# Half as many places for projection slices in the RWKV chunk chain and in the attention core

## What is computed

```python
x = half_swiglu(x, ffn1...)
h = rmsnorm(x, mix_norm)
proj = h @ w_in                    # attention q/k/v of 3 groups | RWKV r,k,v,lora | 2 gates
# attention: 3 dilated groups, 8 heads of 64, QK-norm, ALiBi, softmax, combined by log-sum-exp
# RWKV-7: a scan over time with a 64x64 state per head
#   S = S * w - sk (kk a)^T + v k^T ;  o = S r
x = x + (sigmoid(gA) * (o_attn @ w_branch_attn) + sigmoid(gR) * (o_rwkv @ w_branch_rwkv)) @ w_out
x = half_swiglu(x, ffn2...)
```

## Time and profile before

| | us |
|---|---|
| median of 3 runs | 1797.46 |
| lowest and highest | 1797.06, 1799.55 |
| the profiled execution: device time | 1800.92 |
| its span, first to last instruction | 1799.1 |
| PE busy in it | 1752.8 (97%) |
| PEld busy (weight loads) | 1671.7 (93%) |
| DVE, ACT, POOL busy | 682.3, 631.4, 684.3 |
| mean granted TensorE clock | 0.989 |

### The profile page before, as it was taken

One profiled execution on the slowest core, in us unless ns is written; L12 is line 12 of the kernel. 1 busy time (PEld: TensorE's weight loads), 2 busy tenths in 40 slices (PEclk: granted clock), 3 DMA queues, 4 the chain that ended last, 5 costly groups with the idle time before them and its releaser, 6 DMA issues.

```text
span 1799.1 us, 41814 instructions
## 1 busy us (share of the span) xinstructions
PE 1752.8 (97%) x17024; PEld 1671.7 (93%) x17024; DVE 682.3 (38%) x1113; ACT 631.4 (35%) x825; POOL 684.3 (38%) x816
## 2 busy tenths in 40 slices
PE   6999999999899999999999999999999999999999
PEld 5999999999799999998788989898899999999999
DVE  5222012223764545453573443527444222012210
ACT  5222122233533333332253434435234443144421
POOL 3555445544422222220132323224255555445543
PEclk9999999999899999998899999999999999999999
DMA  4343333332442334231054454546443344333343
GB/s 168 117 128 125 109 114 117 128 129 79 174 146 98 101 108 150 82 113 54 31 216 168 178 180 166 180 142 237 154 158 125 121 124 130 107 123 117 128 134 123
DMA packets 53113, 237.51 MB, mean 132 GB/s; under 512 B 7040, under 2 KB 7680, under 8 KB 51584
## 3 DMA queue, kind: packets, MB, share of 16 engines
q1 hardware_dynamic: 45120, 219.40, 35.8%
q10 hardware_dynamic: 7872, 16.37, 2.5%
HBM read 217.98 MB, written 71.76 MB: 161 GB/s over the span
## 4 chain that ended last, share of the span: by engine, by line
PE 60%; issue 21%; POOL 14%; DVE 2%; ACT 2%; DVEq 0%; POOLq 0%; ACTq 0%
PE ps L355 43%; POOL w_lo L342 14%; PE ps L819 3%; PE ps L1757 1%; PE ps L1934 1%; PE ps L1802 1%; ACT w_hi L335 1%; PE ps L1872 1%; PE ps L1858 1%; PE ps L1842 1%; PE ps L1878 0%; PE ps L965 0%; PE ps L939 0%; PE ps L935 0%; ACT qkv L1545 0%
## 5 line engine op out<-in xcount | busy, mean ns | idle before, releaser
L342 POOL TENSOR_TENSOR w_lo<-w_raw,w_hi 128x256 fp32r<-128x256 f32 (+1 forms) x808 | 678.6, 872 | 1098.8 <-ACT w_hi L335 1098.8
L355 PE MATMUL ps<-h_hi,w_hi 128*128 128x288 f32 x2432 | 546.7, 307 | 22.4 <-POOL w_lo L342 17.8
L355 PE MATMUL ps<-h_lo,w_hi 128*128 128x288 f32 x2432 | 522.6, 297 | 0.0
L355 PE MATMUL ps<-h_hi,w_lo 128*128 128x288 f32 x2432 | 522.5, 297 | 0.0
L355 PEld LDWEIGHTS ps<-h_hi,w_hi 128*128 128x128 f32 x2432 | 393.5, 190 | 45.1 <-issue 25.5
L335 ACT ACTIVATE w_hi<-w_raw 128x1024 fp32r<-128x1024 f32 (+1 forms) x204 | 226.6, 1111 | 586.6 <-PE ps L355 575.8
L355 PEld LDWEIGHTS ps<-h_lo,w_hi 128*128 128x128 f32 x2432 | 394.2, 190 | 0.0
L355 PEld LDWEIGHTS ps<-h_hi,w_lo 128*128 128x128 f32 x2432 | 393.6, 190 | 0.0
L355 PE MATMUL ps<-g_lo,w_hi 128*128 128x288 f32 x704 | 151.2, 296 | 0.0
L355 PE MATMUL ps<-g_hi,w_hi 128*128 128x288 f32 x704 | 151.0, 296 | 0.0
L355 PE MATMUL ps<-g_hi,w_lo 128*128 128x288 f32 x704 | 151.0, 296 | 0.0
(11 more groups left out here) (368 smaller groups left out, 1915.4 us busy)
## 6 DMA issues: line engine op xcount, KB each, us to landing
w_raw<-in_w SPq DMA_DIRECT2D x172, 512.0 KB, 3.3
w_raw<-in_w SPq DMA_DIRECT2D x32, 704.0 KB, 4.1
kv<-in_kc SPq DMA_DIRECT2D x32, 576.0 KB, 6.1
kv<-in_vc SPq DMA_DIRECT2D x32, 576.0 KB, 7.0
cache_out<-in_cache SPq DMA_DIRECT2D x28, 576.0 KB
gates<-gate_out ACTq DMA_DIRECT2D x16, 288.0 KB, 2.6
cache_out<-in_cache SPq DMA_DIRECT2D x8, 480.0 KB
kvT<-qkv ACTq DMA_DIRECT2D x4, 864.0 KB, 4.4
```

Source lines behind the costliest of these rows:

```text
L342: last = nc.gpsimd.tensor_tensor(w_lo[par_][:, c], w_raw[par_][:, c], w_hi[par_][:, c].bitcast(F32), ALU.subtract)
L355: last = nc.tensor.matmul(ps[:, b + c, 0:HC], w[par_][:, wk], a[:, k, c * HC:(c + 1) * HC], start=(first and k == 0), stop=(end and k == n ...
```

## The change

Two tables change. In the chunk chain the eight places of one slice become four places of two: before step 1 and after steps 2, 4 and 6; after steps 1, 3, 5 and 7 nothing is issued. In the attention core, for pairs 0 to 2, slots 0, 2, 4 and 6 get all eight slices of an ahead unit in place of six, and slots 1, 3, 5 and 7 none in place of two. Slots 8 and 9, the whole of pair 3 and every other place stay. No instruction is added or taken away; the order on TensorE alone changes.

```diff
 AHEAD = 5
-SLOTS = ((6, 2, 6, 2, 6, 2, 6, 2, 3, 5),) * 3 + ((4, 4, 4, 4, 4, 4, 4, 4, 0, 0),)
+SLOTS = ((8, 0, 8, 0, 8, 0, 8, 0, 3, 5),) * 3 + ((4, 4, 4, 4, 4, 4, 4, 4, 0, 0),)
 NORMS = (0, 3, 5, 4, 6, 7)
 
 FILL = {"norm": (1, 4, 4, 4), "tokens": (2, 3, 5, 2), "bonus": 1, "products": 2, "level": (5, 3, 3, 3, 3), "mv": 4, "xk": 3,
-        "chunk": (1, 1, 1, 1, 1, 1, 1, 1), "tail": (3, 2)}
+        "chunk": (2, 0, 2, 0, 2, 0, 2, 0), "tail": (3, 2)}
```

## The result

| | median us | lowest, highest | runs |
|---|---|---|---|
| kernel before | 1800.3 | 1794.64, 1806.13 | 20 |
| changed kernel | 1805.01 | 1800.75, 1812.63 | 20 |

The ratio is 1.0026, with a 95% interval of 1.0015 to 1.0037: 2.7 to 6.7 us slower, 4.7 between the medians. The forecast difference of +3.7 us (1.0021) lies inside that interval, but the forecast time, 1801.2 us in a range up to 1804.3, misses the measured 1805.01. The two halves of that sentence are what the rest is about.

The account below looks back on a forecast made before the run. TensorE's own stream was taken to bound the kernel. Three tiles gave -0.2 us and three pairs +3.9, together +3.7 on the median 1797.46: 1801.2 us, range 1797.4 to 1804.3.

Parts of the forecast that it names:

- slot 1: Attention core, mix(0) directly after scores(2): no wait, 0.7 us to spare before scores(3); +0.02 us a pair.
- slot 3: Attention core, mix(2) waits 0.53 us for ScalarE's copy for head 0; with 0.02 for slices, +0.55 us a pair.
- slot 5: Attention core: two consecutive waits on ScalarE's copies, first 0.5 us, second adding 0.4; +0.93 us a pair with slices.
- slot 7: Attention core: the halves, lines 1940 and 1934, touch without slices between; -0.19 us a pair, 0 if the join costs more.
- chunk chain, a tile: Tiles 0 to 2: four appended slices +3.20, removed ones -1.58, -0.63, -1.07; sum -0.08 us, bounds -0.2 and +0.2.
- the join after step 7: Chunk chain, two blocks of the same 64x64 shape meet: 1.08 us for 36 matmuls (1.01 to 1.30), so -1.07.
- Step 6: Chunk chain: after step 5 without its slice, 0.81 us to the next step; a 0.16 wait for VectorE surfaces.
- the case's own bounds: Forecast case, waits show as priced: 1799.3 to 1803 us, chance 0.64, half slower and half same.
- Absorbed: Rival: waits coincide with existing ones, ScalarE answers sooner, or first loads precede the wait's end; 1798.9 us, chance 0.13.
- Faster by saved switches: Rival: each of the vanished runs in chunk chains and core saves idle time at tile-shape changes; 1793.2 us, chance 0.06.
- A further wait: Rival: a wait at slot 1 or for a unit's split weights, 1.2 us a pair or less; 1802 to 1804.5, chance 0.07.
- The clock at slot 7: Rival: clock falls in 5.7 us of lines 1934 and 1940 without a slice; 1803 to 1806 us, chance 0.10.

Follow-up runs that it names:

- e5: Kernel before with only slots 2 and 3 changed to eight slices and none: pairs 53.38, 53.32, 53.36 us, +0.61.
- e6: Kernel before with only slots 4 and 5 changed to eight slices and none: pairs 53.70, 53.72, 53.68 us, +0.96.
- e7: Kernel before with only slots 6 and 7 changed to eight slices and none: pairs 52.54, 52.48, 52.52 us, -0.23.
- e2: Kernel before with only the chunk chain's new places: tiles 19.71 us, median 1798.55, ratio 0.9987 [0.9972, 1.0002].
- e9: Kernel before with slots 4 and 5 at eight and none, ScalarE's copy of ahead unit 2 moved up: pairs 53.08, 52.98, 53.05 us, +0.30.
- e10: Kernel before with slots 2 and 3 at eight and none, ScalarE's copy of turn(2) done twice: pairs 55.56, 55.56, 55.48 us.
- e3: Changed kernel again, on the same chip as its two parts, against the kernel before: median of 10 runs 1803.94 us, ratio 1.0022 [1.0008, 1.0036].

## Why the prediction was right and wrong

**The direction and the size of the difference: right.** Forecast +3.7, measured 4.7 [2.7, 6.7], and +3.7 by the distances: 3 x (54.11 - 52.74) - 3 x 0.15.

**The terms of the sum.**

| | forecast | shown | by |
|---|---|---|---|
| slot 1, a pair | +0.02 | +0.03 | the rest of the whole |
| slot 3 | +0.55 | +0.61 | e5 |
| slot 5 | +0.93 | +0.96 | e6 |
| slot 7 | -0.19 | -0.23 | e7 |
| chunk chain, a tile | -0.08 | -0.15 | changed kernel, e2 |

In slot 3 the latency after the copy was 0.11 and not the 0.06 that a VectorE instruction showed. In the chunk chain the join after step 7 took 1.02 in place of 1.08, and an appended slice 0.79 in place of 0.80. Step 6 took 0.84 after step 5 (567.22 to 568.06), not 0.81, since the step that starts behind slices begins 0.02 slower. Both waits of slot 5 were found where they were put, one behind the other, and e9 took the second away alone. The second was priced a little low: it idled 0.67, of which 0.16 had stood there before, so 0.5 was new and not 0.4. In the prediction the case's own bounds are also added up a little too wide: three tiles of -0.2 to +0.2 and three pairs of 0.9 to 1.6 give 1799.6 to 1802.9, not 1799.3 to 1803.

**The time itself: wrong.** The step that failed is the one that put the difference "on the median: 1797.46 + 3.7 = 1801.2". I read a median of three runs, within 2.5 us of each other, as the kernel's level. Twenty runs gave 1800.3 and a range of 11.5, so the level was 2.8 too low, and 1800.3 + 3.7 would have been 1804.0, inside the range. The warning was on the page: the profiled execution was 3.5 above that median. I noted it and dropped it. The bounds of the forecast's case then were made from the terms of the change alone, with nothing for the level they stood on. A part of the miss is bad luck: of all sets of three that can be drawn from those twenty runs, 6% have a median 2.8 or more off 1800.3. But the runs shown gave no reason to trust the level to a microsecond.

**The rivals.** Absorbed: no, each of twelve pairs is longer. Faster by saved switches: only slot 7 and the end of the chunk chain save one, as those rows said. A further wait: none at slot 1, and none for split weights at slot 2. The clock at slot 7: it didn't fall, in the changed kernel or in e7. But the clock was a rival at the wrong place. In the seven profiles with slot 7 empty it never fell along line 1934; where it fell in a pair, in e10, a wait of 1.2 us had gone before, which is not shown to be the cause. In none of the twelve pairs of the changed kernel did it do so, with waits of 0.58 and of 0.49 and 0.67.

**The rule beside the row.** That a wait holds the load too was right: at 568.06 and at 983.54 the loads idle for VectorE and ScalarE. The pull-ahead of weight loads that the Trainium skill tells of (TensorE: Matmul & The Clock Gate, "Architectural detail") was not seen to pass a wait here.

**Open.** The medians differ by 1.0 more than the distances, and that is within the interval; in the second comparison (e3) they differ by 3.7, as the distances do. No profile showed anything in the changed places that would explain more. The changed kernel's seven slowest timed runs (1808.48 to 1812.63) lie above every run of the kernel before beside them (up to 1806.13), and none of them has a profile. Their mean granted clock over the whole span is on record, 0.988 to 0.990, against 0.989 to 0.992 in the seven fastest (1800.75 to 1802.5). So they stood longer at the lower clock. By the two means, 0.9887 and 0.9909, that is an estimated 4 us of the 9 between the groups. Where in the span it was, and whether the new waits had a part in it, is neither shown nor excluded.

## What to carry to other kernels

Where filling stands between a producer and the block that waits for its result, it is a cover with a size: measure when the result is ready after the block that starts it, and leave at least that much filling there. In this kernel the joins at the other places cost nothing that shows, and where one spared a change of tile shape it gave back 0.2 to 0.3 us. Look for waits that queue on the engine that answers: a copy behind two others can cost more than the one being waited for. Before a forecast is made in absolute time, ask how far whole executions differ, and where the level of the shown runs stands beside the profiled one; for changes of a few us, compare distances between the same instructions rather than spans.

## What the runs showed of the hardware

In one execution the granted clock fell to 0.51 (1.2 GHz) in three pairs, each time about 2 us after a wait of 1.21 or 1.22 us had ended, and in another execution of the same kernel, with a wait of 1.22, it stayed at 1.00. Idle times of 1.53 and 1.6 us at another place left it at 1.00 too, so the wait alone is not shown to bring it down; no pair without such a wait had a fall. Between executions of one kernel the clock's mean over 811 to 830 us was 0.64 and 0.82, for the same work. Switching TensorE between blocks of one full tile shape cost nothing that shows (a load every 0.10 or 0.13 us, before and after), while a block of 128x16 tiles behind one of 64x16 tiles had 0.21 of idle time before it, as did one of 128x128.
